# Two transformer blocks on one core: the next head's projections dealt one to a step, gates in the last heads, weights sent for in another place

## The reference

```
h = rmsnorm(x, norm_g); proj = h @ w_in            # 1024 x 1024 times 1024 x (5632 + 3 * 1024)
aq, ak, av, az, buv, bz, cq, ck, cv, cz, gl = split_cols(proj)
qa, ka = partial_rope(aq), partial_rope(ak)        # rotary: a shuffle, cosine and sine products
p  = softmax(mask(qa @ ka.T * scale))              # two maps per head of branch A
oa = rmsnorm((p[0] - lam * p[1]) @ va, subln_g) * (1 - lam_init)
ya = oa * silu(az)
yb = gelu(u) * (w_causal @ layernorm(gelu(vb)) + b) * silu(bz)
yc = (window attention of cq, ck, cv, three patterns joined) * silu(cz)
merged = sum over branches of sigmoid(gl[n]) * (ys[n] @ w_branch[n])
x = x + merged @ w_out
```

## Time and profile before

| what | value |
|---|---|
| median of 3 runs | 4046.81 us (4042.68 to 4050.09) |
| profiled execution, its own time | 4042.67 us |
| its span in the trace | 4040.9 us |
| TensorE busy | 3743.9 us (93%) in 20820 matmuls |
| TensorE weight loads | 3311.2 us (82%) |
| VectorE busy | 1718.9 us (43%) |
| ScalarE busy | 1265.5 us (31%) |
| GpSimd busy | 1091.6 us (27%) |
| mean granted TensorE clock | 0.964 |
| transfers | 60 GB/s over the span |

### The profile page before, as it was taken

One profiled execution on the slowest core, in us unless ns is written; L12 is line 12 of the kernel. 1 busy time (PEld: TensorE's weight loads), 2 busy tenths in 40 slices (PEclk: granted clock), 3 DMA queues, 4 the chain that ended last, 5 costly groups with the idle time before them and its releaser, 6 DMA issues.

```text
span 4040.9 us, 51127 instructions
## 1 busy us (share of the span) xinstructions
PE 3743.9 (93%) x20820; PEld 3311.2 (82%) x20820; DVE 1718.9 (43%) x3136; ACT 1265.5 (31%) x2868; POOL 1091.6 (27%) x806
## 2 busy tenths in 40 slices
PE   6999998999999899999899999968988998898898
PEld 5787777888887788777778888858988998898898
DVE  6624554433325552455443332554334334333333
ACT  3212443034331211244313333122245422134541
POOL 2533222321113362322231221326310023530002
PEclk9999999999999999999999999979989999998999
DMA  3111110401114212111130112322100031110012
GB/s 113 37 68 63 35 50 32 147 31 42 42 40 176 87 42 78 47 40 44 42 141 29 42 40 79 130 83 65 43 26 19 20 108 56 60 52 13 14 41 95
DMA packets 85195, 243.91 MB, mean 60 GB/s; under 512 B 10720, under 2 KB 25312, under 8 KB 84960
## 3 DMA queue, kind: packets, MB, share of 16 engines
q1 hardware_dynamic: 84960, 240.64, 17.4%
HBM read 190.07 MB, written 50.53 MB: 60 GB/s over the span
## 4 chain that ended last, share of the span: by engine, by line
PE 70%; DVE 14%; ACT 7%; issue 5%; DMA 2%; POOL 2%; SPq 1%; DVEq 0%; POOLq 0%; ACTq 0%
PE pj L1212 27%; PE pS L1212 21%; PE po L1420 4%; PE po L1311 4%; PE pS L1400 3%; PE pS L1402 2%; DVE tmp L2030 1%; PE pS L1282 1%; DVE KK L2042 1%; PE pS L1283 1%; PE pt L1298 1%; DVE tmp L2033 1%; ACT PT L1612 1%; PE pj L1386 1%; DVE tmp L2027 1%
## 5 line engine op out<-in xcount | busy, mean ns | idle before, releaser
L2471 POOL TENSOR_SCALAR Whi<-stage 128x1024 fp32r<-128x1024 f32 (+4 forms) x272 | 277.8, 1021 | 2138.9 <-DMA stage<-wstream 1328.4
L1212 PE MATMUL pj<-Hhi,Whi 128*128 128x512 f32 x1648 | 657.5, 399 | 8.3 <-DVE Hlo L1901 3.3
L1212 PE MATMUL pj<-Hhi,Wlo 128*128 128x512 f32 x1648 | 645.5, 392 | 0.0
L1212 PE MATMUL pj<-Hlo,Whi 128*128 128x512 f32 x1648 | 645.0, 391 | 0.0
L2473 POOL TENSOR_TENSOR Wlo<-stage,Whi 128x1024 fp32r<-128x1024 f32 (+4 forms) x272 | 621.9, 2287 | 22.7
L1212 PEld LDWEIGHTS pj<-Hhi,Whi 128*128 128x128 f32 x1648 | 311.6, 189 | 76.3 <-ACT PT L1612 6.6
L1212 PEld LDWEIGHTS pj<-Hhi,Wlo 128*128 128x128 f32 x1648 | 311.0, 189 | 66.8
L1212 PEld LDWEIGHTS pj<-Hlo,Whi 128*128 128x128 f32 x1648 | 311.6, 189 | 61.4
L1212 PE MATMUL pS<-Hhi,Whi 128*128 128x512 f32 x784 | 312.7, 399 | 12.2 <-DVE Hlo L1901 5.1
L1212 PE MATMUL pS<-Hlo,Whi 128*128 128x512 f32 x784 | 310.0, 395 | 0.0
L1212 PE MATMUL pS<-Hhi,Wlo 128*128 128x512 f32 x784 | 309.5, 395 | 0.0
(11 more groups left out here) (389 smaller groups left out, 7735.8 us busy)
## 6 DMA issues: line engine op xcount, KB each, us to landing
stage<-wstream SPq DMA_DIRECT2D x228, 512.0 KB, 4.3
merged<-Mb SPq DMA_DIRECT2D x32, 512.0 KB, 2.9
Mb<-merged SPq DMA_DIRECT2D x32, 512.0 KB, 5.1
gates<-tmp SPq DMA_DIRECT2D x48, 256.0 KB, 2.2
TH<-gates SPq DMA_DIRECT2D x24, 512.0 KB, 6.1
xres<-X SPq DMA_DIRECT2D x16, 520.0 KB, 5.7
xr<-xres SPq DMA_DIRECT2D x16, 520.0 KB, 4.6
X<-xT SPq DMA_DIRECT2D x16, 256.0 KB, 6.8
```

The costliest lines, as they stand in the source:

```text
L1212: x = pe.e.matmul(ps, w[a][:, v.koff + k * P:v.koff + k * P + P], moving(v.of, b, k, v.t0, v.n), start=k == 0 and i == 0, stop=k == v.K - ...
L2471: pool.e.tensor_scalar(upper, stage, 1.0, 0.0, ALU.mult, ALU.add).then_inc(*pool.tick("whi", c))
```

## The change

A function `plan(j)` replaces the list of fillers in both attentions. It deals the units of a head over the steps: head 0 has z0, v0, v1, z1 and q0 (in A one to each of qb 0 to 4, qb 5 gets none), then k0 alone at qb 6 and q1 alone at qb 7. k1 is held back and comes in the next head's first or second step, behind that head's z0. Heads 1 and 2 have z0, k1, v0, v1, z1, their gates and q0 over qb 0 to 5, k0 at qb 6 and q1 at qb 7; head 3 has z0, k1, z1 and its gates over all eight steps. The units that overwrite q and k now wait on the scores that read the old ones last: q0 on those of qb 3, the rest on those of qb 7. SHARE moves gates to the later heads: A from (1, 1, 1, 1) to (0, 0, 1, 3), C from (2, 2, 2, 2) to (1, 2, 2, 3).

A load of chunk c is now put in the list right behind the last unit that uses chunk c-3, whose room it takes. The "first_weights" units before the second layer's first normalisation and before each normalisation of block 2 are gone, and `ahead` with them. The arithmetic is the same: no matmul is added or removed.

```
-SHARE = {"a": (1, 1, 1, 1), "c": (2, 2, 2, 2)}
+SHARE = {"a": (0, 0, 1, 3), "c": (1, 2, 2, 3)}
...
-        loaded = 0
-        for u, upto in self.upto:
-            last = min(upto, len(self.weights) - 1)
-            u["loads"] = range(loaded, last + 1)
-            loaded = max(loaded, last + 1)
+        at = 0
+        for c in range(len(self.weights)):
+            at = max(at, self.first[c].id if c < NR else self.used_at[c - NR] + 1)
+            self.units[at].setdefault("loads", []).append(c)
...
+        held = []
+        def plan(j):
+            z = z_units(j)
+            others = z[0:1] + held
+            held.clear()
+            g = gates[2 * sum(share[0:j]):2 * sum(share[0:j + 1])]
+            if j == 3:
+                others += z[1:2] + g
+                return [others[len(others) * i // 8:len(others) * (i + 1) // 8] for i in range(8)]
+            read = [[], []]
+            (q0, q1), (k0, k1) = qk_units(j + 1, {("q", 0): read[0], ("q", 1): read[1], ("k", 0): read[1], ("k", 1): read[1]})
+            v = v_units(j + 1)
+            others += v[0:2] + z[1:2] + g + [q0]
+            v[1]["and_then"], z[1]["and_then"] = v[2], v[3]
+            held.append(k1)
+            reads.append(read)
+            n = len(others)
+            return [others[(n * i + 5) // 6:(n * (i + 1) + 5) // 6] for i in range(6)] + [[k0], [q1]]
...
-            if qb == 6 and j < 3:
-                self.fill(len(self.fillers) % 2)
-                rel = [("scores", scored[s + 1].id, m) for m in range(2)]
-                self.fillers = qk_units(j + 1, rel) + self.fillers
-                self.fill(4)
-            if j < 3 or qb in (0, 4) or len(self.fillers) >= 8 - qb:
-                self.fill(1)
+            if j < 3 and qb in (3, 6):
+                reads[j][qb // 6] += [("scores", scored[s + qb // 6].id, h) for h in range(2)]
+            self.run(amid[qb])
             if s:
                 finish(s - 1)
             values(s)
-            if qb == 7:
-                self.fill(99)
```

More of the change, by code:

```diff
@@ L303, in __init__ @@
     def __init__(self):
-        self.units, self.weights, self.upto = [], [], []
+        self.units, self.weights, self.first, self.used_at = [], [], [], {}
         self.bank, self.banks, self.bank_free = 0, WIDE, [None] * 6
@@ L328, in add @@
         if u.opens:
-            u.box["c"] = self.weight(u, u.key, u.ahead)
+            u.box["c"] = self.weight(u.key)
         if u.box is not None:
             u["c"] = u.box["c"]
+            if u.ends:
+                self.used_at[u.c] = u.id
         if u.banked:
@@ L361, in take, with weight @@
         return b, self.bank_free[b]
-    def weight(self, u, key, ahead=None):
+    def weight(self, key):
         self.weights.append(key)
-        i = len(self.weights) - 1
-        self.upto.append((u, i + (NR - 1 if ahead is None else ahead)))
-        return i
+        return len(self.weights) - 1
     def phase(self):
@@ L434, in first_block @@
         self.put("load_x", i=0)
-        self.upto.append((self.put("first_weights"), 1))
+        self.first += [self.put("first_weights")] * 2
         self.put("load_x", i=1)
@@ L467, in norm1 @@
         rs, = self.spread(sums)
-        self.upto.append((self.put("first_weights"), len(self.weights) + NR - 1))
+        if l == 0:
+            self.first.append(self.put("first_weights"))
         self.norm(of, 0, range(2), rs, self.x_ready[0], self.h_free[0])
@@ L529, in gate, with column @@
             return sets
-        def column(make, name, j, toks, emptied, ahead=None):
+        def column(make, name, j, toks, emptied):
             box = {}
             sets = gate(j) if make == "gate_u" else gelu(toks, j)
-            return self.in1(make, l, COL["b" + name] + j * P, j=j, box=box, sets=sets, emptied=emptied, ahead=ahead)
-        v = [column("gelu_v", "v", j, vtok, "gelu", 2 - j if j < 3 else None) for j in range(4)]
+            return self.in1(make, l, COL["b" + name] + j * P, j=j, box=box, sets=sets, emptied=emptied)
+        v = [column("gelu_v", "v", j, vtok, "gelu") for j in range(4)]
         self.together([v[0][0], v[1][0], v[2][0]], self.inside)
@@ L634, in sets_of @@
                 return sets
-            return [u for name in "qk" for u in self.in1("qk", l, COL[br + name] + j * P, name=name, box={}, rel=rel,
-                                                         scale=-SCALE1 if name == "q" else 1.0, sets=sets_of(name),
-                                                         emptied="cosine")]
+            units = [self.in1("qk", l, COL[br + name] + j * P, name=name, box={}, scale=-SCALE1 if name == "q" else 1.0,
+                              sets=sets_of(name), emptied="cosine") for name in "qk"]
+            for pair in units:
+                for u in pair:
+                    u["rel"] = rels[u.name, u.i]
+            return units
         def v_units(j):
@@ L675, in attention @@
         cleared = ("cleared", self.put("clear").id)
-        self.run(qk_units(0, None))
+        (q0, q1), (k0, k1) = qk_units(0, {(x, i): None for x in "qk" for i in range(2)})
+        self.run([q0, q1, k0, k1])
         self.run(v_units(0))
@@ L750, in attention @@
             if qb == 0:
[L751 to L755, removed]
+                amid = plan(j)
             if more:
@@ L867, in fourier_pool @@
         self.put("small_in", l=l)
-        f = [self.in2("f_copy", key("f", i), x=i, box={}, emptied="f_copy", ahead=NR - 1 - i) for i in range(2)]
-        p = [self.in2("p_copy", key("p", i), x=i, box={}, emptied="p_copy", ahead=i * (NR - 1)) for i in range(2)]
+        f = [self.in2("f_copy", key("f", i), x=i, box={}, emptied="f_copy") for i in range(2)]
+        p = [self.in2("p_copy", key("p", i), x=i, box={}, emptied="p_copy") for i in range(2)]
         self.together([f[0][0], f[1][0], p[0][0]], self.inside)
@@ L894, in fourier_pool @@
                                  lts=((0, 1, 2), (3, 4))[piece], free=ps_free[2 * part:2 * part + 2])
-                    u["c"] = self.weight(u, u.dkey)
+                    u["c"] = self.weight(u.dkey)
+                    self.used_at[u.c] = u.id
             u = self.put("unfold", kc=kc, k0=k0, n=n, even=("dft", u.id - 2), odd=("dft", u.id), osb_free=osb_free,
```

5 lines of the change are left out of this document (2 added, 3 removed).

## The result

The changed kernel takes 4312.6 us (median of 4, 4311.0 to 4318.2) against 4045.8 before: ratio 1.066, 95% interval [1.064, 1.068]. It is slower, as forecast, but by 267 us where the sum said 179, and above the range.

The account below looks back on a forecast made before the run. TensorE's stream was taken as the path, so only its waits and lower clock count. Attentions +92 us a layer, +184 for two, and -5 for weights sent sooner gave 4042.7 + 179 = 4222, said as 4220 us; range 4110 to 4290.

Parts of the forecast that it names:

- the sum: Whole kernel: attentions +92 us a layer, +184 for two, weights sent sooner -5; 4042.7 + 179 = 4222, said as 4220.
- A lone q or k unit: In both attentions, 5.40 (q) or 4.95 us (k) on VectorE delays the next turns: net +33 per A, +37 per C.
- q0 in A: At qb 5 of A, turns come after 6.03 us and TensorE's work covers 3.30: a stall of 2.7 us.
- In the attentions a load one unit sooner brings nothing: Inside A and C, the earlier weight load gains nothing, since TensorE's largest waits there are others.
- the sharing with VectorE: At q1 and k1, GpSimd's split of the next chunk slows VectorE's sine product: 2.1 us each.
- Weights outside the attentions: Earlier loads save 13 us, clock included, at normalisations; splits cost 8 in the branch B stages: net -5.
- The wait of 9.57 us: TensorE's longest wait for split weights behind a normalisation, given as 9.6 us, removed almost whole by the earlier load.
- The clock: TensorE's granted clock drops after stalls: +11 us per A and +11 per C; A's from 0.97 to 0.93 or so.
- rival 3: Clock stays low for one or two of four steps at each of 12 attention boundaries: 4270 to 4370 us; chance 0.12.
- Rival 1: In the attentions, TensorE's work hides the lone units and boundary waits go: faster, about 3958 us; chance 0.07.
- its LDWEIGHTS share: Bound on A: its 245.4 us of weight loads at C's LDWEIGHTS-busy share of 0.825 would need 297 us.

Follow-up runs that it names:

- e13: Changed kernel with loads outside the attentions placed as before and, inside them, GpSimd's splits behind the small softmax-scale operations: 4202.6 us, ratio 1.039.
- e5: Changed kernel with, in the attentions, GpSimd's weight splits issued behind the step's two small softmax-scale operations instead of ahead: 4227.5 us, ratio 1.045.
- e2: Changed kernel with the weight loads outside the four attentions put back where they were before, first_weights units included: 4278.0 us, ratio 1.059.
- e9: Changed kernel with pt read-out first, e5's and e2's edits, q0 at qb 5, k0 and q1 at qb 6, k1 at qb 7: 4049.8 us, ratio 1.002.

## Why the prediction was wrong in size

- **A lone q or k unit stalls TensorE: right.** q1 at 8.08 us after L1336 (8.13 forecast), k0's waits 3.3 and 1.8 (3.5 and 2.0), in A q1 5.6 (5.5) and k1 5.8 to 6.3 (6.0), in C k1 5.3 to 6.0 (6.3) and q1 3.7 (4.0). C grew by 49 and 46 for 48. e13, in which the splits run beside the units in C alone, costs 158, where the sum has 184 - 25 = 159.
- **q0 in A: wrong, 2.7 forecast, 6.3 measured, and the end of A.** The step that failed is the one on loads: "In the attentions a load one unit sooner brings nothing". It costs, since the split is ahead of the scale's small operations in GpSimd's queue, twice in a row or waiting for its transfer. I had printed that very order ahead of the prediction and priced only the sharing with VectorE. e5 took 41 us from each A; 12 of it (six times 1.95, read off q1 and k1) is the sharing that the sum had, and the other 29, 58 for two, are missing from the sum: up to 21.5 each as idle time in GpSimd's queue, and the clock behind it.
- **Weights outside the attentions: wrong in sign.** Forecast -5 with the branch B stages, measured +26 outside the attentions, and the rest falls back by 29 when it is undone (e2). The wait of 9.57 us is gone as said, but the two waits for zlo behind GpSimd's pooled sums alone grew by 9.7. Where the other part of the 26 arose was not traced.
- **The clock: too small a term, but not rival 3.** Mean granted clock 0.938 against 0.964; A's fell to 0.89 where 0.93 was forecast. In the four attentions the length grew by 67 us beyond the idle time (A by 20 and 18, C by 16 and 13), where the sum had 44 and rival 3 at least 96. The clock came back between the stalls. Windows from q1's stall in A's first boundary on:

```profile
457.50:471.80 14.30, 8.74 (x36) 6.98 (x34) 6.53 (x13) 4.56 (x13) 3.26 (x3) 0.76 0.11 37
471.80:479.60 7.80, 7.08 (x36) 5.76 (x36) 3.94 (x13) 3.32 (x10) 0.85 (x3) 1.00 0.00 0
479.60:495.80 16.20, 10.37 (x42) 8.21 (x40) 8.94 (x16) 4.36 (x11) 4.53 (x4) 0.79 0.09 33
495.80:523.00 27.20, 27.19 (x156) 23.33 (x154) 11.99 (x25) 11.89 (x31) 9.48 (x10) 1.00 0.11 39
```

  0.24 x 14.3 and 0.21 x 16.2 are 3.4 us a stall, twice the 1.7 of the sum. Some of it lies in the idle time itself and costs nothing: in C the clock lost 26 us (0.06 x 439.5) and the length grew only 16 more than the idle time did. The result lies within rival 3's times by chance: the clock cost less than rival 3 needs, and the rest came from GpSimd's queue and the loads outside.
- **The misses add up**: the two A were 59 above their forecast (e5 gives 58 of it back), the stages outside the attentions 31, the two C 1 below: 89, and the profiled executions lie 89 further apart than the sum had (268 less 179). A slip of 4 us stands in the sum as well: the profiled execution is 4 us below the median, which makes 4226 and not 4220; the result is above the range with either.
- **Rival 1** needed 6 us of cover behind a unit; there were 1.2 (k1 in A) to 4.8 (q0 in C). The best A found (e9's second, 308.8 us) is still above the 297 that its LDWEIGHTS share gave.

## What to carry to other kernels

What covers a filler's tail on an in-order engine is not the step but whatever follows it on TensorE before the next dependence: put work of several microseconds behind another filler's matmuls, not in front of a step's short work. When a wait is moved in one queue, look for what it passes in the next (VectorE, then ScalarE here) before counting a gain. A load placed one unit sooner is also a pair of GpSimd instructions placed ahead of others, and where they wait for a transfer, the others wait as well.

## What the runs showed of the hardware that was not expected

A GpSimd split held the VectorE instruction with both inputs in SBUF that started after it, and not the one that had started before: the sine product, at 457.13 and 0.03 us ahead of the split's L2490, took its 0.68 us, and L2050 at 457.92 took 2.65. In the earlier trace rows, with the split 0.15 us ahead, it was the sine product that took 2.79. And the granted clock was at 1.00 again in the steps after stalls of 5.6 and 5.8 us, with a loss of 3.4 us each.
